# Latent attention two heads at a time with side-by-side value products, and modulation products for two weight blocks at once

## The reference, cut to what matters

```python
def mla_mixer(h, h_c, ...):                      # 16 heads, 96 = 64 + 32 rotated columns, values 64
    q = rms_norm(q_lat, g_qa) @ w_qb             # (rows, 16, 96)
    kv = rms_norm(kv_lat, g_kva) @ w_kvb         # (rows, 16, 64 + 64)
    ...
    s = einsum(q, k) * scale; p = softmax(s); o = einsum(p, v)
    return gated(o, gate), gated(o_c, gate_c)    # o * silu(gate)
```

## Time and profile before

| | |
|---|---|
| time, median of 3 runs | 1667.3 us |
| lowest, highest | 1667.1, 1669.59 us |
| the profiled execution: span | 1666.1 us |
| instructions | 28604 |
| TensorE / VectorE / ScalarE / GpSimd busy | 1582.5 / 1006.0 / 696.4 / 915.0 us |
| mean granted TensorE clock | 0.983 |

### The profile page before, as it was taken

How to read it: one execution, slowest core, us unless ns; L and a number is a source line. 1 busy time by engine, 2 the same in 40 slices (tenths; PEclk the granted TensorE clock), 3 DMA queues, 4 the chain that set the end, 5 groups by cost and what they waited for, 6 DMA issues and landing times.

```text
span 1666.1 us, 28604 instructions
## 1 busy us (share of the span) xinstructions
PE 1582.5 (95%) x11752; PEld 1282.3 (77%) x11752; DVE 1006.0 (60%) x1308; ACT 696.4 (42%) x1210; POOL 915.0 (55%) x722
## 2 busy tenths in 40 slices
PE   6999888999999999999989999999989999999887
PEld 5677787678888888878877777768877888888775
DVE  5699785746565540052465756664766665656566
ACT  4653775333222220042336565661154344444562
POOL 5354787838999999964550321346524444444152
PEclk9999999999999999999999999999899999999998
DMA  5221104422322243341120000003321101111211
GB/s 194 76 90 62 54 4 156 152 102 76 101 101 87 89 159 119 116 150 51 51 76 1 26 1 26 1 4 148 127 90 51 48 29 51 51 51 51 102 51 51
DMA packets 18881, 126.15 MB, mean 76 GB/s; under 512 B 2096, under 2 KB 2352, under 8 KB 4304
## 3 DMA queue, kind: packets, MB, share of 16 engines
q1 hardware_dynamic: 18624, 124.02, 21.2%
q10 hardware_dynamic: 144, 0.52, 0.1%
HBM read 122.43 MB, written 2.10 MB: 75 GB/s over the span
## 4 chain that ended last, share of the span: by engine, by line
PE 54%; issue 19%; POOL 12%; DVE 9%; ACT 4%; DMA 1%; POOLq 0%; ACTq 0%; SPq 0%; DVEq 0%
POOL w_hi L672 8%; PE banks L1324 5%; PE banks L1303 4%; POOL w_lo L663 4%; PE banks L1481 4%; PE banks L1484 4%; PE banks L1482 4%; PE banks L1186 3%; PE banks L1191 3%; PE banks L1187 3%; PE banks L1536 2%; PE banks L781 2%; PE banks L782 2%; PE banks L783 2%; PE banks L1516 2%
## 5 line engine op out<-in xcount | busy, mean ns | idle before, releaser
L672 POOL TENSOR_TENSOR w_hi<-raw,der 128x512 fp32r<-128x512 f32 x296 | 333.8, 1138 | 419.8 <-PE banks L1484 186.9
L663 POOL TENSOR_TENSOR w_lo<-raw,w_hi 128x512 fp32r<-128x512 f32 x336 | 479.6, 1440 | 61.9 <-ACT w_hi L1624 61.6
L781 PE MATMUL banks<-h_hi,w_hi 128*128 128x512 f32 x464 | 184.2, 397 | 0.3 <-DVEq L2308 0.3
L782 PE MATMUL banks<-h_lo,w_hi 128*128 128x512 f32 x464 | 180.7, 389 | 0.0
L783 PE MATMUL banks<-h_hi,w_lo 128*128 128x512 f32 x464 | 180.6, 389 | 0.0
L1481 PE MATMUL banks<-h_hi,w_hi 128*128 128x512 f32 (+1 forms) x384 | 146.3, 381 | 0.1
L1482 PE MATMUL banks<-h_lo,w_hi 128*128 128x512 f32 (+1 forms) x384 | 131.0, 356 | 0.0
L2145 ACT ACTIVATE dP<-banks,der 128x768 f32<-128x768 f32 x64 | 57.8, 902 | 160.2 <-DVE der L2981 160.2
L725 POOL TENSOR_TENSOR Of<-Of,Ls 128x768 f32<-128x768 f32 x8 | 14.7, 1834 | 186.6 <-DVE Ls L2783 186.6
L1484 PE MATMUL banks<-h_hi,w_lo 128*128 128x512 f32 (+1 forms) x384 | 116.1, 356 | 0.0
L781 PEld LDWEIGHTS banks<-h_hi,w_hi 128*128 128x128 f32 x464 | 87.1, 188 | 25.9 <-issue 7.5
(11 more groups left out here) (514 smaller groups left out, 3856.9 us busy)
## 6 DMA issues: line engine op xcount, KB each, us to landing
raw<-in_stream SPq DMA_DIRECT2D x84, 1024.0 KB, 4.9
ada_raw<-in_ada_w SPq DMA_DIRECT2D x18, 1024.0 KB, 7.1
raw<-in_ada_w SPq DMA_DIRECT2D x4, 1024.0 KB, 4.8
xT<-in_x_t SPq DMA_DIRECT2D x2, 1024.0 KB, 6.6
xT<-in_x_t SPq DMA_DIRECT2D x1, 2048.0 KB, 7.9
ada_end<-in_ada_w SPq DMA_DIRECT2D x2, 1024.0 KB, 5.9
out_t<-z SPq DMA_DIRECT2D x8, 256.0 KB, 2.1
ctxT<-in_ctx_t SPq DMA_DIRECT2D x1, 1024.0 KB, 6.9
```

Source lines behind the costliest of these rows:

```text
L663: return pool.tensor_tensor(lo[:, h, part(i), :], raw_tiles(half)[:, part(i), :], hi[:, h, part(i), :], ALU.subtract)
L672: pool.tensor_tensor(hi[:, h, part(i), :], raw_tiles(half)[:, part(i), :], one, ALU.mult).then_inc(hi_done, 1)
L781: pe.matmul(banks[b][:, :], hi, tile(rhs_hi, k), start=(at_k == 0), stop=False)
L782: pe.matmul(banks[b][:, :], hi, tile(rhs_lo, k), start=False, stop=False)
```

## The change

**Attention.** Both heads of a pair are worked at once. The 14 score steps of a pair alternate between its heads (`scores(i)`: pair, step j, head). A weight buffer holds both heads' weights of a step, and there are three (`Pf`, 3 x 2 x 512, was 4 x 512). A value step, at every second score step, makes two products with 64 columns of V each, one to rows 0 to 63 and one to rows 64 to 127 of one bank. V holds no ones. The sums are made apart: GpSimd adds the seven buffers up (`add_part`, VectorE's `last_part` for the last pair), TensorE multiplies the result by ones, 64 columns a head (`sums_x`, `sums_c`), and `inverse` reads them from PSUM. `Of` and `Ls` have one buffer instead of two, QHI and QLO have four instead of three. Order and places change:

```diff
-        def values(h, j):
+        def values(p, j):
...
+            v, weighed = VV[p % 2], Pf[:, (N_S * p + j) % N_PF, :, :]
             if j < 6:
-                mm = pe.matmul(pairs[1][:, 0, :], v[:, j, :], Pf[:, i % 4, :], start=(j == 0), stop=(j == 5), skip_group_check=True)
+                for e in range(2):
+                    mm = pe.matmul(banks[2][HEAD[e], :], v[:, j, HEAD[e]], weighed[:, e, :], start=(j == 0), stop=(j == 5), skip_group_check=True)
...
+        def sums_x(p):
+
+            pe.wait_ge(*added(p, 5))
+            if p:
+                pe.wait_ge(sums_inverse, 3 * p)
+            for e in range(2):
+                mm = pe.matmul(banks[sum_bank(p, 0)][HEAD[e], :], ones[:, HEAD[e]], Sx[:, e, :], start=True, stop=True, skip_group_check=True)
+            mm.then_inc(sums_full.sem, 1)
...
+        TOP_SLOTS = [1, 2, 3, 4, 5, 7, 8, 9, 10, 11]
+        for p in range(N_PAIRS):
+            more = p < LAST_PAIR
+            for s in range(N_STEP):
+                if s == 6 and more:
+                    row(2 * p + 2)
+                if s == 12 and more:
+                    row(2 * p + 3)
+                if N_STEP * p + s + 1 < N_STEP * N_PAIRS:
+                    scores(N_STEP * p + s + 1)
+                if s == 0 and p == 0:
+                    key(1)
+                if more and s in (1, 2):
+                    query(2 * p + 3, s - 1)
+                if more and s in TOP_SLOTS:
+                    t = TOP_SLOTS.index(s)
+                    tops(2 * p + 2 + t // 5, t % 5)
+                if s == 2 and p:
+                    sums_x(p - 1)
+                if s == 8 and p:
+                    sums_c(p - 1)
+                if more and s in (5, 6):
+                    value_tokens(p + 1, range(3 * (s - 5), 3 * (s - 5) + 3))
+                if s in (8, 9) and p + 2 < N_PAIRS:
+                    query(2 * p + 4, s - 8)
+                if s == 12 and p + 2 < N_PAIRS:
+                    key(p + 2)
+                if s % 2:
+                    values(p, s // 2)
```

ScalarE's list for one pair (`weigh_keys` is the exponential), and VectorE's:

```diff
+            for s in range(N_STEP):
+                weigh_keys(N_STEP * p + s)
+                if s == 0 and p:
+                    output_c(p - 1)
...
+                if s == 0 and more:
+                    key_hi(p + 1, 1)
+                if s == 3 and more:
+                    query_copy(2 * p + 3)
+                if s == 4 and more:
+                    query_hi(2 * p + 3)
...
+                if s == 12 and more:
+                    row_copy(2 * p + 3)
+                if s == 12:
+                    output_x(p)
+                if s == 13 and further:
+                    query_hi(2 * p + 4)
+                    key_hi(p + 2, 0)
...
+        for p in range(LAST_PAIR):
+            a, b, after = 2 * p + 2, 2 * p + 3, 2 * p + 4
+            top(a, 0)
+            top(a, 1)
+            rope_query(b)
+            rope_query_sum(b)
+            top(a, 2)
+            if p:
+                inverse(p - 1, 0)
+            top(a, 3)
+            top(a, 4)
+            query_lo(b)
+            if p:
+                inverse(p - 1, 1)
+            for t in range(3):
+                top(b, t)
+            if p:
+                inverse(p - 1, 2)
+            if after < A_HEADS:
+                rope_query(after)
+            top(b, 3)
+            if after < A_HEADS:
+                rope_query_sum(after)
+            top(b, 4)
+            if after < A_HEADS:
+                query_lo(after)
+                key_lo(p + 2)
```

```diff
-                for k in range(KT):
-                    for q in range(4):
-                        cols = ada_source(b)[:, k, :].rearrange("p (t q c) -> p t q c", t=2, q=4)[:, :, q, :]
-                        mm = pe.matmul(banks[ADA_BANK[g]][32 * q:32 * q + 32, 64 * a:64 * a + 64].rearrange("p (t c) -> p t c", t=2),
-                                       (silu_pad if g < ADA_LATE else silu_last)[:, k, :], cols, start=(k == 0), stop=(k == KT - 1))
+            for k in range(KT):
+                for q in range(4):
+                    mm = pe.matmul(banks[ADA_BANK[g]][32 * q:32 * q + 32, 0:P].rearrange("p (a t c) -> p a t c", a=2, t=2),
+                                   (silu_pad if g < ADA_LATE else silu_last)[:, k, :], ada_moving(g, k, q), start=(k == 0), stop=(k == KT - 1))
-        CHAIN_ADA = {1: 2, 2: 3, 4: 4, 5: 5}
+        CHAIN_ADA = {2: 1, 5: 2}
...
-            ada_blocks([14])
...
-            ada_blocks([15])
+            ada_product(7)
...
-            ada_blocks((16, 17, 18, 19))
+            ada_product(8)
+            ada_product(9)
...
-            ada_blocks([20 + qt])
+            if qt % 2 == 0:
+                ada_product(ADA_LATE + qt // 2)
```

More of the change, by code:

```diff
@@ L590, in _ @@
         weights(2, out0)
-        for b in range(2):
-            sp.wait_ge(split_full, out0 + b - 1)
-            ada_block(b)
+        for n in (out0, out0 + 1):
+            sp.wait_ge(split_full, n - 1)
+            ada_block(half_of(n))
         weights_behind(out0, 0)
@@ L720, in _ @@
         assert (before - first) % 2 == 0
[L722 to L733, removed]
-                n += 1
+        split(BLK1, 0, BLK1 // 2)
@@ new lines, in _ @@
+        n = BLK1 + 1
+        for p in range(LAST_PAIR):
+            first_half = p % 2 == 0
+            split_steps(n, 0 if first_half else 6, 2)
+            if not first_half:
+                n += 1
+            for j in (1, 2, 3):
+                add_part(p, j)
+                if first_half and j < 3:
+                    split_steps(n, j + 1, 1)
+            if p:
+                finish(p - 1, 0)
+            add_part(p, 4)
+            if p:
+                finish(p - 1, 1)
+            add_part(p, 5)
+            if first_half:
+                split_steps(n, 4, 1)
+            add_part(p, 6)
+            if first_half:
+                split_steps(n, 5, 1 if p < LAST_PAIR - 1 else 3)
@@ L760, in _, with project @@
         pe.wait_ge(s_first, 32)
-        def project(bank_of, half, n, frees, rhs_hi, rhs_lo, ready=None, order=range(KT), between=(), ready_base=0, small=None, middle=None):
+        def project(bank_of, half, n, frees, rhs_hi, rhs_lo, ready=None, order=range(KT), ready_base=0, small=None, middle=None):
             def tile(src, k):
@@ L1351, in _ @@
         key(0)
-        mla_in(10, range(0, 4))
-        value_tokens(0, range(6))
-        mla_in(10, range(4, KT))
-        for k in range(2):
-            query(1, k)
+        for k in range(KT):
+            mla_in(10, [k])
+            if k == 1:
+                for q in range(2):
+                    query(1, q)
+            if k == 4:
+                value_tokens(0, range(6))
+            if k >= 4:
+                tops(0, k - 4)
         for k in range(KT):
             mla_in(11, [k])
-            if k in (0, 2, 3, 5, 6):
-                tops(0, (0, 2, 3, 5, 6).index(k))
@@ L1361, in _ @@
-        row(0)
-        scores(0, 0)
-        for h in range(A_HEADS):
-            nxt, after = h + 1, h + 2
-            for j in range(N_S):
-                if j == 5 and nxt < A_HEADS:
-                    row(nxt)
-                if j < 6:
-                    scores(h, j + 1)
-                elif nxt < A_HEADS:
-                    scores(nxt, 0)
-                if j < 5 and nxt < A_HEADS:
-                    tops(nxt, j)
-                if after < A_HEADS:
-                    if j in (0, 2):
-                        query(after, j // 2)
-                    if h % 2 == 0 and j == 4:
-                        key(after // 2)
-                    if h % 2 and j in (4, 5):
-                        value_tokens(after // 2, range(3 * (j - 4), 3 * (j - 4) + 3))
-                values(h, j)
@@ L1382, in _ @@
-        pe.wait_ge(exp_done, N_S * A_HEADS)
+            if k == 0:
+                tops(0, 4)
+            if k == 2:
+                row(0)
+            if k >= 3:
+                tops(1, k - 3)
+        scores(0)
+        for k in range(2):
+            query(2, k)
+        row(1)
+        TOP_SLOTS = [1, 2, 3, 4, 5, 7, 8, 9, 10, 11]
[27 more added lines that the diff above has]
+                    values(p, s // 2)
@@ L1400, in last_norm @@
             pe.wait_ge(z_acc, Z_ADDED + 5)
-            pe.matmul(banks[5][:, :], ones, zacc[:, 0:T], start=True, stop=False)
+            pe.matmul(banks[5][:, :], ones, zacc[:, :], start=True, stop=False)
             token_sums(3, zacc, True, False)
@@ L2077, in _ @@
+        output_c(LAST_PAIR)
         for m in range(KT):
@@ L2790, in _ @@
         rope_query_sum(1)
+        query_lo(1)
         for t in range(5):
             top(0, t)
+        for t in range(5):
+            top(1, t)
+        rope_query(2)
+        rope_query_sum(2)
         dve.wait_ge(block_done, BLK_LAST + 1)
         fill(1)
-        query_lo(1)
         for e in range(2):
```

432 lines of the change are left out of this document (234 added, 198 removed).

## The result

The changed kernel takes 1719.8 us, median of 4 runs (1718.7 to 1722.8), against 1667.3 (1667.1 to 1669.6) for the kernel before: ratio 1.0317, 95% interval 1.0303 to 1.0330. The profiled execution took 1718.72 with a span of 1716.9, 50.8 more than before. I had predicted 1690.7 and at most 1708: the direction was right, the size 29 us too small (27.4 by the spans, 1716.9 against a forecast of 1689.5).

The account below looks back on a forecast made before the run. TensorE, busy 95% of the span, was taken as the bound. Terms −13.3 − 6.5 + 13.4 + 29.3 + 5.7 − 3.2 + 4 − 6 = +23.4 us gave 1690.7 against a median of 1667.3; range 1650 to 1708.

Parts of the forecast that it names:

- the value products: Attention on TensorE: 56 paired steps at 0.86 + 0.34 a visit, 67.2 us where 112 steps took 96.3.
- Rival 2: Attention: visits to 64-column tiles cost nothing, 24.5 us less, about 1666, no change; chance 0.07.
- The first pair: Start of attention: waits of about 1.8 and 7, clock drop 2.5, maxima 2.1; +13.4 us together.
- A: TensorE's wait between a pair's key and the next query, for KLO: 2.5 us in each of pairs 1 to 6.
- B: TensorE's wait at the maxima of a pair's first head, behind VectorE's list: 1.95 us a pair.
- C: TensorE's wait at the maxima of a pair's second head: 1.4 us in pairs 1 to 5, 1.0 in pair 6.
- The modulation: Half the instructions, each twice as wide: "issue" gaps of 8.9 us go, product itself gains nothing; −6 us, bounds 0 and −10.
- Rival 1: Attention: TensorE stays the bound and the waits are hidden; −26 us, 1641; chance 0.25.
- six gaps A: Waits between key and next query, each followed by products at 1.2 GHz: 0 to 12 us, taken as +4.
- 33.46 − 0.35 − 1.66: TensorE's work per pair: old query-to-query period, less its key-to-query wait, less the products-and-sums gain (−13.3 over the stage).
- the last pair ... 0: End of attention: VectorE takes over the additions, its long queue covered by tile 0's products (7.3 us); 0, bounds 0 and +5.
- the waits' sizes: Attention: three waits a pair, together 5.85 us, +29.3 over pairs 1 to 5; first pair's maxima 2.1.

Follow-up runs that it names:

- ada_only: Kernel before with only the modulation in pairs of blocks, attention as before: 1664.8 us against 1668.1, ratio 0.9972.
- last_pair_mended: Changed kernel with orders inside pairs mended, GpSimd adding in the last pair too, and that pair's rounding, splitting and sums reordered: 1666.4 us, ratio 0.9982.
- dummy_a: Changed kernel plus seven unread 512-column products in the wait between a pair's key and the next query: 1709.1 us, ratio 1.0233.
- inverse_moved: Changed kernel with only VectorE's order in a pair changed (inverses, rotation and its sum moved): 1696.8 us, ratio 1.0170.
- key_first: Changed kernel with the key ahead of the query on ScalarE and VectorE at a pair's end: 1703.3 us, ratio 1.0217.
- best_half_visits: Changed kernel with mended orders, GpSimd adding in the last pair too, and two value steps per visit (four visits a pair): 1684.0 us, ratio 1.0115.

## Why the prediction was right in kind and wrong in size

**Right: the value products.** A visit was to cost 0.86 + 0.34. The changed kernel, around one value step:

```profile
913.07 0.27 PE L1347 MATMUL banks<-KHI,QHI 128*128 128x256 f32 x1
913.27 1.08 PE L1397 MATMUL banks<-Pf,V 128*64 128x512 f32 x4
...
914.28 0.50 PE L1376 MATMUL banks<-QHI,KHI 128*128 128x512 f32 x1
...
914.62 0.39 PE L1376 MATMUL banks<-QLO,KHI 128*128 128x512 f32 x1
```

From 913.07 to 914.62 are 1.55; less 0.11 and 0.24 for the two full products, 1.20. Rival 2 (free visits) is refuted by this and by the 0.30 to 0.42 above.

**Right: the places.** All waits that I named are there, with the releasers named. The first pair has 1.90 and 6.64 for 1.8 and 7. A is 1.79 for 2.5, B 2.15 for 1.95, C 2.41 for 1.4 (its rotation's sum took 2.04 beside GpSimd; I had 0.7): 6.35 for 5.85. B and C came near with a slip in them: the durations that I named for VectorE's two lists add up to some 0.3 less than the 7.1 and 5.35 that I used. Wait A ends as I had it, with ScalarE's second half of KHI and VectorE's two steps (chain of waits):

```profile
941.95 0.82 ACT KHI L2089
942.77 0.02 issue
942.79 0.95 DVE KLO L2865
943.75 0.97 DVE KLO L2865
944.73 0.14 issue
944.86 0.47 PE banks L1260
```

**The modulation: right in size, partly by luck.** −6 forecast, −5.3 in the span of ada_only and −4.6 by its ratio. But the reason was to be that "issue", 8.9 us, goes. It went, and other waits came (83.1 us in all for 83.6); the gain is 2.2 us less loss by the clock and 2.6 less of TensorE's own work, which was to gain nothing. And it lies elsewhere: 6.7 us ahead of the latent attention (I had 3.9), with 1.4 lost again behind it (I had 2.1 won).

**Rival 1 is not what happened, and its price was wrong too.** It was to be lost from 2.6 us of wait a pair on, and there were 6.36. With most of them hidden (14 us of waits are left in the stage, 52 in the changed kernel) the whole change is worth −3 us (last_pair_mended), or −7 with four visits, not −26: besides those 14, TensorE's own work in a pair fell less than I had it.

**Wrong, first: the clock, "six gaps A of 2.5 at up to 2 us each are 0 to 12, I take +4".** The stage loses 18.9 us to it against 2.6 before, +16; with the first pair's 2.5, and 2.5 taken back at the start, I had +4. So 12 of the 27 us in the span are this term, the largest. I priced each gap by itself, by the products that followed single gaps of 1.9 us and more in the earlier trace rows. Here five waits of 1.0 to 1.8 stand in each period, and the half clock came behind any of them, in one pair behind C, in another behind B:

```profile
1119.00:1123.00 4.00, 1.97 (x10) 1.46 (x11) 3.40 (x4) 1.83 (x3) 3.41 (x3) 0.98 0.00 0
1123.00:1127.00 4.00, 4.00 (x18) 2.27 (x18) 3.34 (x3) 0.00 (x0) 0.89 (x1) 0.50 0.00 0
1127.00:1131.00 4.00, 4.00 (x19) 3.46 (x17) 0.00 (x0) 2.25 (x4) 1.69 (x1) 0.67 0.00 0
```

dummy_a shows the cause, not only the coincidence: the same waits with TensorE busy in one of them, and 10 us are back. Why some periods have such a stretch and others with the same waits have none stays open.

**Wrong, second: TensorE's own work.** I had 33.46 − 0.35 − 1.66 = 31.45 a period. Measured: 38.70 − 6.36 = 32.34 (and 32.34 in inverse_moved, 32.36 in key_first, with shorter waits). A part of this is that I took 0.35 off for a wait of which the same column of the table has 0.10:

```profile
947.38:980.84 33.46, 33.36 (x161) 24.36 (x162) 22.30 (x24) 19.79 (x35) 3.66 (x2) 1.00 0.00 0
```

Like for like, TensorE's own work fell by 33.36 − 32.34 = 1.02 a pair where I had 1.66. Seven pairs × 0.64 is some 4 us. Most of it is that I took a value step of before for 0.86, read from the chain, where starts in the timeline give 14 value and 14 score steps 21.2 us together, not 14 × (0.86 + 0.69) = 21.7.

**Wrong, third: "the last pair ... 0".** It cost some 5 us of waits. ScalarE's rounding of tile 6 waited 3.38 for GpSimd's gate with exponentials behind it, and VectorE was full until 1176. ScalarE's row, and TensorE's waits:

```profile
1162.06 0.84 ACT L2128 ACTIVATE OT_HI<-gate_s 128x768 fp32r<-128x768 f32 x1 [3.38 <-POOL gate_s L779]
```

```profile
1163.44 1.70 PE L1397 MATMUL banks<-Pf,V 128*64 128x512 f32 x4 [2.78 <-ACT Pf L2112]
1167.50 1.08 PE L1401 MATMUL banks<-Pf,V 128*64 128x256 f32 x8 [0.78 <-ACT Pf L2112]
...
1187.81 0.51 PE L1260 MATMUL banks<-OT_HI,w_hi 128*128 128x512 f32 x1 [1.59 <-DVE OT_LO L2901]
```

I had counted TensorE's cover (7.3 us of product), but not the length of VectorE's queue: from 1157 to 1176 it has no gap:

```profile
1164.48 2.06 DVE L2894 TENSOR_TENSOR Sx<-Sx,Pf 128x1024 f32<-128x1024 f32 x1
1166.46 2.01 DVE L2901 TENSOR_TENSOR OT_LO<-gate_s,OT_HI 128x768 fp32r<-128x768 f32 x1
1168.39 2.05 DVE L2894 TENSOR_TENSOR Sx<-Sx,Pf 128x1024 f32<-128x1024 f32 x1
```

**Wrong, fourth: the waits' sizes**, 6.36 for 5.85 in five periods, and 5.0 for the 2.1 of the first pair's maxima (38.36 less 33.32 in the table), 5.5 us together. By the spans the account is: clock 12, own work 4, waits of the attention 8 (3.6 in the last pair, 5.5 as just said, less 1.5 elsewhere), and 4 behind the attention (1.6 in waits of the output product, nearly 2 of the clock) less 1 won ahead of it, 27 for a miss of 27.4. Each term is known to about 1. The other 1.7 of the 29 us is that the median lay 2.9 above the profiled span, not 1.2.

## What to carry to other kernels

Where one engine is full and its order is written by hand, moving work off it pays only if every list behind it is drawn up again: the same arithmetic took 1719.8 us in one order and 1666.4 in another, with a few steps handed from VectorE to GpSimd. Price a wait on TensorE twice, once for itself and once for the clock: here one edit to VectorE's list brought 13 us of waits and 7 of clock. A visit to narrow tiles has its own price (0.30 to 0.42 us here), so put two steps in each before counting on the overlap, and look whether this opens a wait elsewhere: in best_half_visits one wait of 1.53 us a pair, with the clock behind it, cost more than the visits gave.

## What the runs showed of the hardware that I had not expected

Waits of 1.0 to 1.8 us, five in 38.7, brought TensorE to 1.2 GHz in some periods and not in others of the very same instructions (43.4, 41.5, 38.7 and 41.4 us in a row), and in best_half_visits a wait of 1.53 us did so in four pairs of seven; filling one of the five with products that nobody reads made the kernel 10.7 us faster. That a program gets faster by doing more on its fullest engine is something that I had not allowed for.
